# Feed-forward: how the 42 modulation chunks computed by GpSimd are summed over partitions, and how many may wait for their sum

## The chip, the cores and the metric

One core of a Trainium2 chip runs the whole program. The metric is the device time of one execution in microseconds (us). The engines are TensorE (PE in the profile, PEld for its weight loads), VectorE (DVE), ScalarE (ACT), GpSimd (POOL) and SyncE (SP), which issues most loads.

## The reference, cut to what matters

The model is two layers of a first block (token mixers, then a feed-forward with a short convolution) followed by two layers of a second block, on 512 tokens of 1024 features. Every layer is modulated by vectors that come from a product of a conditioning vector with a wide matrix:

```
mod = (cond @ w_ada[l] + b_ada[l])[:, None, :]
sh1, sc1, g1, sh2, sc2, g2 = jnp.split(mod, 6, axis=-1)
h = _rmsnorm(x, norm1_w[l]) * (1.0 + sc1) + sh1
x = x + g1 * _token_mixers(h, ...)
h = _rmsnorm(x, norm2_w[l]) * (1.0 + sc2) + sh2
x = x + g2 * _conv_ffn(h, ...)      # gelu(conv(h @ w_up) gate) * value @ w_down
```

`w_ada` is 1024 x 6144 for each layer of the first block and 1024 x 3072 for each of the second. The kernel cuts these products into chunks of 256 output columns. A few more products of the same kind ("shift" chunks) multiply the shift vector with the first columns of the next weight.

## The kernel before, in words

**Layout.** Activations are kept transposed: features on the 128 partitions, 512 tokens in the free dimension, 8 tiles `k` of 128 features. Every big product is made of three matmuls on rounded halves: an operand is split into a rounded high part (`hh`, `wh`, `fh`; by ScalarE) and the rounded rest (`hl`, `wl`, `fl`; by VectorE), and `thrice` issues high x high, high x low, low x high. In the profile all matmuls of these have line L560.

**Weights.** A piece of 1 MB of weights is loaded by SyncE into `raw` (2 buffers), ScalarE writes `wh`, VectorE writes `wl` by a subtraction of `wh` from `raw` (2 buffers each). TensorE then uses it for about 11 us. `Order.use(key)` marks the start of the use of a piece; it also places, in all engines' queues, the split of the next piece (`split_one`) and what comes with it.

**Feed-forward.** `order_ffn` writes the order by hand: 34 pieces, `up(0, 8)`, `up(8, 8)`, `down(0, 8)`, `up(16, 6)`, `down(1, 8)`, `down(2, 6)`. An up piece gives two channel tiles, in turn for the gate (`ug`) and the value (`uv`). Each tile goes through ScalarE (centre tap) and two VectorE instructions (outer taps, reading PSUM), then gelu on ScalarE, the product `ug<-ug,uv` on VectorE, and its split into `fh` and `fl`. A feed-forward begins with `order_early`: the first piece is multiplied with rows that are not yet normalised (`fh`, `fl` of `xT`), while VectorE and ScalarE make the normalised rows: for each of 8 tiles VectorE scales (`uv<-xT,acoef,rr`), ScalarE writes `hh`, VectorE writes `hl` (`hl<-uv,mod,hh`). TensorE's second piece waits for `hl` tile by tile.

**Modulation chunks.** During the two feed-forwards 42 chunks (25 in the first, 17 in the second) are computed by GpSimd, as unit `adap`. For each half of the 1024 rows: a multiplication by the conditioning vector (L1951, 128x1024), an addition (L1953, 128x512), then 128x256 additions (L1958, L1960, L1962) that leave in `adaacc` 128 partial sums for each of 256 columns. Behind each half it issues the load of the same half of the next chunk (L1934). The first chunk of a feed-forward waits for the last attention step of the block before (`s3`), so GpSimd begins well ahead of the feed-forward itself. A chunk's first write of `adaacc` (L1958) waits for the sum of the chunk that held the place before; there are two places.

**Sums.** Unit `adasum`: TensorE multiplies each half of `adaacc` as stationary operand with one column of ones (two float32 matmuls that write one column each), and VectorE adds the bias (`mod<-ps,sv`, 128x2). `Order.late` lists chunks whose sum is not yet placed. `split_one` places a sum when more than one chunk is late, `use` places all that were late at the use before, and `down` places what is left ahead of the first and the third down stage and at the end.

Of the kernel before, what the change touches and what calls it, by code (L numbers as in the profile page):

```python
# [107 lines left out]
class Memory:  # L108
    def __init__(self, nc, ctx):
        base = (nc.sbuf_base + 31) // 32 * 32  # L110
        top = nc.sbuf_usable_end // 32 * 32
        at = [base]
# [82 lines left out]
        self.strewn = [sb(f"strewn{i}", [128, 4, 256])[:, :, :] for i in range(2)]  # L195

# [43 lines left out]
    def mixer(self, nm, c):  # L240
# [6 lines left out]
        return y[:, c, :], high, low[:, c, :]  # L247

# [68 lines left out]
class Order:  # L317


    def __init__(self, plan):  # L320
        self.plan, self.units, self.split, self.used = plan, [], 0, 0
        self.late, self.old = [], 0
# [7 lines left out]

    def sums(self, n=None):
        for _ in range(len(self.late) if n is None else n):
            self.run(("adasum", self.late.pop(0)))
        self.old = 0

    def split_one(self):
# [5 lines left out]
        if self.plan[j]["kind"] == "ada":  # L342
# [3 lines left out]
            if len(self.late) > 1:  # L346
                self.run(("adasum", self.late.pop(0)))
                self.old = max(self.old - 1, 0)
# [7 lines left out]
    def use(self, key, alone=False):  # L356
# [6 lines left out]
        self.sums(self.old)  # L363
# [4 lines left out]
        while not alone and self.split <= then:  # L368
            self.split_one()
        return j  # L370
# [167 lines left out]
def tensor_program(e, X):  # L538
# [77 lines left out]
    def adasum(chunk_):  # L616
        b = take("side", ("ada", chunk_))
        acc = M.adaacc[X.acc[chunk_]]
# [300 lines left out]
def scalar_program(e, X):  # L919
# [47 lines left out]

    def split(j):
# [286 lines left out]
    def mixer_split(l, nm, c):  # L1255
        y, high, _ = M.mixer(nm, c)
        go.wait_ge(*at("gated", l, nm, c))
        if nm == "c":
            if c == 1 and l == 0:
                go.wait_ge(*at("sums", (2, 1, 11)))  # L1260
# [54 lines left out]
    parts = {"start": start, "loaded": loaded, "split": split, "sq": square, "sqf": first_square, "mod": modulate, "rms": inv_rms, "row": row,  # L1315
# [73 lines left out]
def vector_program(e, X):  # L1389
# [76 lines left out]

    def adasum(chunk_):
        which, l, j = chunk_
        if which == "shift":
# [10 lines left out]
    def ada_quick(n):  # L1480

        chunk_ = X.first[n]["chunk"]
        b = bank("ada", chunk_)
        sums, own = (b[:, c:c + 256].rearrange("p (x t) -> p x t", x=2) for c in (0, 256))
        dst, bias = M.mod1[:, 2 * chunk_[2]:2 * chunk_[2] + 2], M.vec("bada", 2 * chunk_[2], 2)
        go.wait_ge(*at("sums", chunk_))
        tt(own, sums, M.cst[:, C_ID:C_ID + 128].rearrange("p (x t) -> p x t", x=1).broadcast_to([128, 2, 128]), ALU.mult).then_inc(
            *up("dve_mod"))
        go.wait_ge(*last("dve_mod"))
        e.tensor_reduce(dst, own, mybir.AxisListType.X, ALU.add).then_inc(*up("dve_mod", ("out", ("ada", chunk_))))  # L1490
        go.wait_ge(*last("dve_mod"))
# [399 lines left out]
    parts = {"start": start, "loaded": loaded, "split": split, "ada0": ada_first, "adaq": ada_quick, "adaqm": ada_quick, "ada": ada, "adasum": adasum, "sq": square, "sqf": first_square,  # L1891
# [350 lines left out]
def order_ffn(o, l):  # L2242
# [19 lines left out]
    def down(gr, n, norm=None):  # L2262
        settle()
        if gr == 0:
            o.sums()
        if norm:
            tag = ("m1", 1) if l == 0 else ("m3", 0)
            o.sums()
            o.put("es", tag)
            o.put("lnexp")  # L2270
        for c in range(4):
            j = o.use(("down", l, gr, c))
            for x in range(2):
                o.put("down", l, gr, n, 2 * c + x, j)
# [330 lines left out]
```

## Time and profile before

| | |
|---|---|
| median of 3 runs | 2823.48 us (2821.91 to 2830.59) |
| the profiled execution | 2823.8 us, span 2822.0 us |
| TensorE busy | 2693.7 us (95% of the span) |
| VectorE, ScalarE, GpSimd busy | 1818.2, 1152.3, 693.9 us |
| granted TensorE clock, mean | 0.975 |
| chain that ended last | TensorE 85%, VectorE 7%, ScalarE 4% |

The first feed-forward lies at about 410 to 783 us of the span, the second at about 1134 to 1503 us. Where TensorE is busy without a gap, time changes only by the TensorE instructions that are added or removed and by waits that come to it from other engines.

### The profile page before, as it was taken

The page shows a single profiled execution, that of the slowest core. Times are in us where ns is not written, and L with a number is a line of the kernel's source. Part 1 is how long each engine was busy: PE and PEld are TensorE (multiplying, and loading weights), DVE is VectorE, ACT ScalarE, POOL GpSimd, SP SyncE. Part 2 cuts the span into 40 slices and gives each one's busy share as a digit, 9 for nine tenths or more (in the row PEclk, how much of TensorE's full clock was granted, in tenths as well). Part 3 has the DMA queues.
Part 4 walks back from the last instruction along what each step waited for, and adds up shares of the span by engine and source line. Part 5 has one row for each costly group of instructions (what it writes and reads, how often), then busy time and mean ns, then how long its engine had stood idle before and what let it go on. Part 6 is the DMA issues. An engine that isn't in the chain of part 4 may idle for free.

```text
span 2822.0 us, 36991 instructions
## 1 busy us (share of the span) xinstructions
PE 2693.7 (95%) x14886; PEld 2163.9 (77%) x14886; DVE 1818.2 (64%) x2968; ACT 1152.3 (41%) x1900; POOL 693.9 (25%) x514
## 2 busy tenths in 40 slices
PE   6999899999999998999998999989999999999997
PEld 5877578888878676888886878767687788777686
DVE  7789668867577676876558768645436557545434
ACT  3143544323243454533224463344324464444422
POOL 0000047988700004356540032000010132000110
PEclk9999999999999999999999999999899999999999
DMA  8353034554432212444433435221232323221231
GB/s 270 119 144 103 29 120 149 165 173 160 138 118 57 70 44 90 132 137 149 145 109 107 157 99 158 77 64 56 72 97 79 99 61 94 79 86 53 75 97 60
DMA packets 281114, 302.59 MB, mean 107 GB/s; under 512 B 9968, under 2 KB 263024, under 8 KB 280944
## 3 DMA queue, kind: packets, MB, share of 16 engines
q1 hardware_dynamic: 267568, 250.21, 28.4%
q0 software_dynamic: 13088, 49.55, 5.3%
q8 instruction: 118, 1.93, 0.3%
q10 hardware_dynamic: 288, 0.47, 0.0%
q14 instruction: 52, 0.43, 0.0%
HBM read 289.97 MB, written 2.10 MB: 103 GB/s over the span
## 4 chain that ended last, share of the span: by engine, by line
PE 85%; DVE 7%; ACT 4%; DMA 1%; issue 1%; SPq 0%; POOL 0%; DVEq 0%; ACTq 0%
PE ps L560 84%; PE ps L768 2%; DVE wl L1398 1%; DVE hl L1404 1%; DVE adaacc L1404 1%; DMA raw<-in_w_in 1%; DVE rawt L1404 0%; ACT wh L926 0%; DVE recat L1696 0%; ACT recat L926 0%; ACT hh L926 0%; DMA stage<-in_w_ada 0%; DMA t1s<-rawt 0%; ACT att_s L926 0%; ACT att_p L926 0%
## 5 line engine op out<-in xcount | busy, mean ns | idle before, releaser
L560 PE MATMUL ps<-hh,wh 128*128 128x512 f32 x2208 | 890.9, 403 | 24.8 <-DVE wl L1398 10.3
L560 PE MATMUL ps<-hh,wl 128*128 128x512 f32 x2208 | 868.0, 393 | 0.0
L560 PE MATMUL ps<-hl,wh 128*128 128x512 f32 x2208 | 867.2, 393 | 0.0
L1398 DVE TENSOR_TENSOR wl<-raw,wh 128x2048 fp32r<-128x2048 f32 (+3 forms) x234 | 501.2, 2150 | 208.1 <-ACT wh L926 207.8
L560 PEld LDWEIGHTS ps<-hh,wh 128*128 128x128 f32 x2208 | 417.6, 189 | 138.1 <-issue 39.6
L560 PEld LDWEIGHTS ps<-hh,wl 128*128 128x128 f32 x2208 | 417.6, 189 | 92.3
L560 PEld LDWEIGHTS ps<-hl,wh 128*128 128x128 f32 x2208 | 418.2, 189 | 81.2
L926 ACT ACTIVATE wh<-raw 128x2048 fp32r<-128x2048 f32 (+3 forms) x234 | 369.9, 1591 | 188.3 <-PE ps L560 172.8
L560 PE MATMUL ps<-fh,wh 128*128 128x512 f32 x432 | 171.6, 397 | 0.0
L560 PE MATMUL ps<-fh,wl 128*128 128x512 f32 x432 | 168.3, 390 | 0.0
L560 PE MATMUL ps<-fl,wh 128*128 128x512 f32 x432 | 168.1, 389 | 0.0
L1951 POOL TENSOR_TENSOR strewn<-strewn,cond 128x1024 f32<-128x1024 f32 x80 | 161.6, 2020 | 7.2 <-DMA strewn<-in_w_ada 5.4
L926 ACT ACTIVATE rawt<-ps 128x512 f32<-128x512 f32 (+1 forms) x106 | 63.1, 597 | 244.9 <-PE ps L560 244.7
L1404 DVE SCALAR_TENSOR_TENSOR xT<-ps,mod,xT 128x512 f32<-128x512 f32 x80 | 59.6, 748 | 146.8 <-PE ps L560 146.8
L1953 POOL TENSOR_TENSOR strewn<-strewn 128x512 f32<-128x512 f32 x84 | 150.2, 1788 | 6.6
L1977 POOL TENSOR_TENSOR merged<-merged,rawt 128x512 f32<-128x512 f32 x32 | 41.7, 1316 | 439.6 <-DVE rawt L1404 439.6
L1912 POOL DMA_DIRECT2D gbias<-in_gb x6 | 3.5, 577 | 552.7 <-DVE stt L1735 457.3
L560 PE MATMUL ps<-wh,hh 128*128 128x256 f32 x448 | 129.5, 289 | 3.3 <-DVE apad L1398 3.3
L560 PE MATMUL ps<-wh,hl 128*128 128x256 f32 x448 | 127.3, 284 | 0.0
L560 PE MATMUL ps<-wl,hh 128*128 128x256 f32 x448 | 127.3, 284 | 0.0
L560 PEld LDWEIGHTS ps<-recq,reck 64*128 64x128 f32 x1536 | 100.7, 200 | 29.0 <-issue 15.2
L560 PE MATMUL ps<-recq,reck 64*128 64x64 f32 (+2 forms) x1536 | 110.4, 295 | 7.2 <-DVE reck L1398 4.5
(291 smaller groups left out, 4157.0 us busy)
## 6 DMA issues: line engine op xcount, KB each, us to landing
raw<-in_w_in SPq DMA_DIRECT2D x75, 1024.0 KB, 5.4
raw<-in_w_up SPq DMA_DIRECT2D x46, 1024.0 KB, 5.1
strewn<-in_w_ada POOLq DMA_DIRECT2D x80, 512.0 KB, 4.1
raw<-in_w_ada SPq DMA_DIRECT2D x24, 1024.0 KB, 5.2
raw<-in_w_in SPq DMA_DIRECT2D x44, 512.0 KB, 5.1
raw<-in_w_out SPq DMA_DIRECT2D x16, 1024.0 KB, 5.1
raw<-in_w_down SPq DMA_DIRECT2D x16, 1024.0 KB, 5.2
stage<-in_w_ada SPq DMA_DIRECT2D x8, 1024.0 KB, 11.6
```

Source lines behind the costliest of these rows:

```text
L560: return e.matmul(o, a, b, start=start, stop=stop, skip_group_check=True)
L768: m = e.transpose(b[:, o:o + 128], S[:, 128 * x:128 * x + 128], M.ident)
L926: return e.activation(o, a, f, **k)
L1398: return e.tensor_tensor(o, a, b, op)
L1404: return e.scalar_tensor_tensor(out=o, in0=a, scalar=s, in1=b, op0=op0, op1=op1)
L1912: e.dma_start(M.Gb[h], X.T["gb"][2 * c + h, :, :]).then_inc(*X.tally.up16("bias_in", ("bias", l, c)))
L1951: e.tensor_tensor(v, v, weights, ALU.mult).then_inc(*up("pool_ada"))
L1953: e.tensor_tensor(v[:, 0:2, :], v[:, 0:2, :], v[:, 2:4, :], ALU.add).then_inc(*up("pool_ada"))
L1977: e.tensor_tensor(M.merged[:, o, :], M.merged[:, o, :], raw[:, :], ALU.add).then_inc(*up("pool_merge", ("merged", l, nm, o)))
```

## The change

The 42 chunks of the feed-forwards (`strewn`) are summed in another way. ScalarE copies the chunk's `adaacc` into a rounded `acc_high` (new unit `accs`), VectorE subtracts that from `adaacc` and leaves the rounded rest in the same place. TensorE multiplies a stationary matrix of minus ones with both (two matmuls with 256 moving columns each), so that each partition of the bank holds all 256 negated sums. VectorE multiplies them by the identity, reduces each row and subtracts the result from the bias. GpSimd has four places instead of two; the chunks that VectorE computes elsewhere keep two. The order of the sums changes: a chunk is halved (`halve`) at the end of a `use` when at least two chunks are late, and summed at the next `use`; nothing is flushed at the start of a down stage but what that stage needs. The chunks are strewn over 30 pieces instead of 32.

```diff
         self.strewn = [sb(f"strewn{i}", [128, 4, 256])[:, :, :] for i in range(2)]
+        self.acc_high = [sb(f"acchigh{i}", [128, 256], F32R) for i in range(2)]
+        self.adamore_r = rounded("adamore_r", [128, 512], at[0])
+        self.adaacc += [sb(f"adamore{i}", [128, 256]) for i in range(2)]
...
+    def halve(self):
+        if self.late and self.late[0] in self.strewn and self.late[0] != self.halved:
+            self.halved = self.late[0]
+            self.run(("accs", self.late[0]))
+
+    def sum_one(self):
+        self.halve()
+        self.run(("adasum", self.late.pop(0)))
...
     def split_one(self):
-            if len(self.late) > 1:
-                self.run(("adasum", self.late.pop(0)))
+            if len(self.late) > (3 if self.plan[j]["chunk"] in self.strewn else 1):
+                self.sum_one()
                 self.old = max(self.old - 1, 0)
...
     def use(self, key, alone=False):
         self.used += 1
-        self.sums(self.old)
+        if self.late and self.late[0] in self.strewn:
+            if self.halved == self.late[0]:
+                self.sum_one()
+        else:
+            self.sums(self.old)
         self.old = len(self.late)
         while self.split <= j:
             self.split_one()
...
+        if len(self.late) > 1:
+            self.halve()
         return j
...
     def adasum(chunk_):                      # TensorE
         b = take("side", ("ada", chunk_))
+        if chunk_ in X.strewn:
+            go.wait_ge(*at("rounded"))
+            go.wait_ge(*at("acc_low", chunk_))
+            high, low = M.acc_parts(X.acc[chunk_])
+            mm(b[:, 0:256], M.cst_r[:, C_NONE:C_NONE + 128], high, True, False)
+            mm(b[:, 0:256], M.cst_r[:, C_NONE:C_NONE + 128], low, False, True).then_inc(*up("pe_ada", ("sums", chunk_)))
+            return
...
+    def acc_split(chunk_):                   # ScalarE
+        go.wait_ge(*at("acc", chunk_))
+        act(M.acc_parts(X.acc[chunk_])[0], M.adaacc[X.acc[chunk_]][:, :], ACT.Copy).then_inc(*up("act_acc", ("acc_high", chunk_)))
...
+    def acc_split(chunk_):                   # VectorE
+        high, low = M.acc_parts(X.acc[chunk_])
+        go.wait_ge(*at("acc_high", chunk_))
+        tt(low, M.adaacc[X.acc[chunk_]][:, :], high.bitcast(F32), ALU.subtract).then_inc(*up("dve_acc", ("acc_low", chunk_)))
+
+    def own_sums(chunk_, dst, eye=M.ident):
+        sums, own, mask = M.diagonals(bank("ada", chunk_), eye)
+        go.wait_ge(*at("sums", chunk_))
+        tt(own, sums, mask, ALU.mult).then_inc(*up("dve_mod"))
+        go.wait_ge(*last("dve_mod"))
+        e.tensor_reduce(dst, own, mybir.AxisListType.X, ALU.add).then_inc(*up("dve_mod", ("out", ("ada", chunk_))))
+        go.wait_ge(*last("dve_mod"))
+
+    def strewn_sum(chunk_):
...
+        own_sums(chunk_, dst[:, col:col + 2])
+        tt(dst[:, col:col + 2], M.vec(bias, col, 2), dst[:, col:col + 2], ALU.subtract).then_inc(*up("dve_mod", ("mods", chunk_)))
...
     def down(gr, n, norm=None):
         settle()
-        if gr == 0:
-            o.sums()
+        while gr == 0 and any(c[:2] == (1, l) and c[2] >= 20 for c in o.late):
+            o.sum_one()
         if norm:
-            o.sums()
+            while any(c[:2] == ((1, 1) if l == 0 else (2, 0)) and c[2] < 8 for c in o.late):
+                o.sum_one()
...
                 o.put("down", l, gr, n, 2 * c + x, j)
+                if norm and c < 3 and x == 0:
+                    o.halve()
...
-        for n, c in enumerate(chunks):
-            self.acc[c], self.acc_before[c] = n % 2, chunks[n - 2] if n > 1 else None
+        ring, holder = [0, 0], {}
+        for c in chunks:
+            turn = 1 if c in self.strewn else 0
+            n = ring[turn] % (4 if turn else 2)
+            ring[turn] += 1
+            self.acc[c], self.acc_before[c], holder[n] = n, holder.get(n), c
...
-            (lambda: ffn(0), ada(1, 0, (5,)) + ada(1, 1, (1, 0, 2, 4)) + shift("m1", 1) + ada(1, 1, (3,)), 0, 32),
+            (lambda: ffn(0), ada(1, 0, (5,)) + ada(1, 1, (1, 0, 2, 4)) + shift("m1", 1) + ada(1, 1, (3,)), 0, 30),
-            (lambda: ffn(1), ada(1, 1, (5,)) + ada(2, 0, (1, 0, 2)) + shift("m3", 0), 0, 32),
+            (lambda: ffn(1), ada(1, 1, (5,)) + ada(2, 0, (1, 0, 2)) + shift("m3", 0), 0, 30),
```

## Rows read from the trace of the kernel before

**Rows 1.** The page: TensorE's busy time, and the other engines'.

```profile
PE 2693.7 (95%) x14886; PEld 2163.9 (77%) x14886; DVE 1818.2 (64%) x2968; ACT 1152.3 (41%) x1900; POOL 693.9 (25%) x514
```

**Rows 2.** Stretches: length; busy PE, PEld, DVE, ACT, POOL; clock; DMA share, GB/s.

```profile
456.00:592.00 136.00, 136.00 (x620) 112.92 (x618) 112.56 (x94) 50.95 (x61) 116.73 (x83) 1.00 0.51 167
834.00:845.00 11.00, 9.14 (x65) 8.66 (x65) 7.50 (x14) 2.78 (x3) 0.00 (x0) 0.69 0.35 95
```

**Rows 3.** The timeline of TensorE before and after one sum: start, duration, instruction.

```profile
456.23 0.39 PE L560 MATMUL ps<-hh,wl 128*128 128x512 f32 x1
...
459.68 0.39 PE L560 MATMUL ps<-hh,wh 128*128 128x512 f32 x1
```

**Rows 4.** The timeline of TensorE where matmuls of 256 columns follow ones of 512.

```profile
2246.42 0.39 PE L560 MATMUL ps<-hh,wl 128*128 128x512 f32 x1
...
2247.10 0.39 PE L560 MATMUL ps<-hh,wl 128*128 128x512 f32 x1
2247.32 0.28 PE L560 MATMUL ps<-wh,hh 128*128 128x256 f32 x1
2247.44 0.28 PE L560 MATMUL ps<-wl,hh 128*128 128x256 f32 x1
```

**Rows 5.** The timeline of GpSimd, 398 to 443 us; in brackets idle before and releaser.

```profile
400.47 1.63 POOL L1953 TENSOR_TENSOR strewn<-strewn 128x512 f32<-128x512 f32 x1
432.73 0.73 POOL L1958 TENSOR_TENSOR adaacc<-strewn 128x256 f32<-128x256 f32 x1 [30.64 <-PE ps L560]
...
439.09 1.06 POOL L1962 TENSOR_TENSOR adaacc<-adaacc,strewn 128x256 f32<-128x256 f32 x1
...
441.26 1.91 POOL L1951 TENSOR_TENSOR strewn<-strewn,cond 128x1024 f32<-128x1024 f32 x1
```

**Rows 6.** GpSimd's additions of 128x512, whole span: duration ns min/median/max.

```profile
L1953 POOL TENSOR_TENSOR strewn<-strewn x84: 1282/1627/3242, 373.0 to 1460.0; 128x512 f32<-128x512 f32 x84
```

**Rows 7.** The timeline of VectorE at the first feed-forward's start.

```profile
412.43 2.29 DVE L1398 TENSOR_TENSOR wl<-raw,wh 128x2048 fp32r<-128x2048 f32 x1 [1.05 <-ACT wh L926]
414.64 1.41 DVE L1404 SCALAR_TENSOR_TENSOR uv<-xT,acoef,rr 128x512 f32<-128x512 f32 x2
...
424.14 1.63 DVE L1404 SCALAR_TENSOR_TENSOR hl<-uv,mod,hh 128x512 fp32r<-128x512 f32 x2
```

**Rows 8.** The timeline of TensorE, the end of the same stretch.

```profile
425.83 0.50 PE L560 MATMUL ps<-hh,wh 128*128 128x512 f32 x1
...
432.08 0.95 PE L560 MATMUL ps<-cst,adaacc 128*128 128x1 f32 x8
```

**Rows 9.** The timeline of VectorE while GpSimd works, beside rows 5.

```profile
438.58 0.97 DVE L1398 TENSOR_TENSOR ug<-ug,uv 128x512 f32<-128x512 f32 x1
439.48 1.22 DVE L1398 TENSOR_TENSOR fl<-ug,fh 128x512 fp32r<-128x512 f32 x1
...
440.76 4.57 DVE L1398 TENSOR_TENSOR wl<-raw,wh 128x2048 fp32r<-128x2048 f32 x1
```

**Rows 10.** VectorE's instructions on `xT`, whole span: duration ns min/median/max.

```profile
L1404 DVE SCALAR_TENSOR_TENSOR xT<-ps,mod,xT x80: 733/750/752, 374.6 to 2806.9; 128x512 f32<-128x512 f32 x80
...
L1404 DVE SCALAR_TENSOR_TENSOR fl<-xT,acoef,fh x40: 737/747/2754, 376.7 to 2174.1; 128x512 fp32r<-128x512 f32 x40
L1404 DVE SCALAR_TENSOR_TENSOR uv<-xT,acoef,rr x16: 741/744/747, 414.6 to 1147.3; 128x512 f32<-128x512 f32 x16
```

**Rows 11.** The timeline of all engines at the second feed-forward's start.

```profile
1147.93 1.63 DVE L1404 SCALAR_TENSOR_TENSOR hl<-uv,mod,hh 128x512 fp32r<-128x512 f32 x2
...
1155.87 0.50 PE L560 MATMUL ps<-cst,adaacc 128*128 128x1 f32 x4
...
1156.51 0.74 POOL L1958 TENSOR_TENSOR adaacc<-strewn 128x256 f32<-128x256 f32 x1 [30.53 <-PE ps L560]
```

**Rows 12.** The timeline of TensorE, its one long wait in an up stage.

```profile
445.47 0.47 PE L560 MATMUL ps<-hh,wh 128*128 128x512 f32 x1 [1.40 <-DVE wl L1398]
```

**Rows 13.** VectorE by group, 10 to 60 us: busy, mean ns of one.

```profile
L1398 DVE TENSOR_TENSOR ps<-ps,cst 128x256 f32<-128x256 f32 x4 | 1.7, 426 | 0.0
```

More of the change, by code:

```diff
@@ L247, in mixer, with acc_parts, diagonals @@
         return y[:, c, :], high, low[:, c, :]
+    def acc_parts(self, n):
+        low = self.adaacc_r if n < 2 else self.adamore_r
+        return self.acc_high[n % 2][:, :], low[:, 256 * (n % 2):256 * (n % 2) + 256]
+    def diagonals(self, b, eye):
+        sums, own = (b[:, c:c + 256].rearrange("p (x t) -> p x t", x=2) for c in (0, 256))
+        return sums, own, eye.rearrange("p (x t) -> p x t", x=1).broadcast_to([128, 2, 128])
     def split_parts(self, p):
@@ L321, in __init__ @@
         self.plan, self.units, self.split, self.used = plan, [], 0, 0
-        self.late, self.old = [], 0
+        self.late, self.old, self.halved = [], 0, None
+        self.strewn = {p["chunk"] for p in plan if p["strewn"]}
         self.main_free, self.side_free, self.split_end = [0.0], [0.0], {}
@@ L1313, in index_scores @@
             *up("act_index", ("out", ("ts", l, i, h)), ("relu", l, i, h)))
-    parts = {"start": start, "loaded": loaded, "split": split, "sq": square, "sqf": first_square, "mod": modulate, "rms": inv_rms, "row": row,
+    parts = {"start": start, "loaded": loaded, "split": split, "accs": acc_split, "sq": square, "sqf": first_square, "mod": modulate, "rms": inv_rms, "row": row,
              "er": early_row, "em": early_mend, "z": z, "q": q, "iv": iv, "g": g, "qk": qk, "a": a, "zs": gates, "rd": rec_diagonal, "rl": rec_level, "ra": rec_across, "ro": rec_out,
@@ L1465, in ada @@
         products(p["chunk"], M.piece(M.raw[p["slot"]], p, 0))
+    def acc_split(chunk_):
[10 more added lines that the diff above has]
+    def strewn_sum(chunk_):
+        which, l, j = chunk_
+        go.wait_ge(*at("rounded"))
+        if which == "shift":
+            dst = M.shifted((l, j))
+            own_sums(chunk_, dst)
+            ts(dst, dst, -1.0, None, ALU.mult).then_inc(*up("dve_mod", ("mods", chunk_)))
+            return
+        dst, bias, per = (M.mod1, "bada", 48) if which == 1 else (M.mod2, "bada2", 24)
+        col = l * per + 2 * j
+        own_sums(chunk_, dst[:, col:col + 2])
+        tt(dst[:, col:col + 2], M.vec(bias, col, 2), dst[:, col:col + 2], ALU.subtract).then_inc(*up("dve_mod", ("mods", chunk_)))
     def adasum(chunk_):
         which, l, j = chunk_
+        if chunk_ in X.strewn:
+            strewn_sum(chunk_)
+            return
         if which == "shift":
@@ L1482, in ada_quick @@
         chunk_ = X.first[n]["chunk"]
-        b = bank("ada", chunk_)
-        sums, own = (b[:, c:c + 256].rearrange("p (x t) -> p x t", x=2) for c in (0, 256))
         dst, bias = M.mod1[:, 2 * chunk_[2]:2 * chunk_[2] + 2], M.vec("bada", 2 * chunk_[2], 2)
[L1486 to L1491, printed above, removed]
+        own_sums(chunk_, dst, M.cst[:, C_ID:C_ID + 128])
         tt(dst, dst, bias, ALU.add).then_inc(*up("dve_mod", ("mods", chunk_)))
@@ L2404, in __init__ @@
         self.first = first_chunks(T)
+        self.strewn = {p["chunk"] for p in self.plan if p["strewn"]}
         self.order = make_order(Order(self.plan), self.first)
```

6 lines of the change are left out of this document (3 added, 3 removed).

## The prediction

> **What bounds the kernel.** I read the page first: TensorE is busy 95% of the span [rows 1]. The waits within the feed-forwards come next; in the table by stretch TensorE is busy for all of the 136 us of the up pieces, while VectorE has 23.4 us to spare and GpSimd 19.3 [rows 2]. So here a change counts for what it adds to or takes from TensorE's own queue, and for what it makes late enough to stop TensorE. For the first I read the timeline of TensorE around one sum. For the second I read three timelines side by side at the start of a feed-forward, because that is the one place there where VectorE sets TensorE's pace: the last `hl` tile is written by 425.77 (424.14 plus 1.63) and the matmul that needs it starts at 425.83; TensorE then has the rest of that piece before it and comes to the next one, with its first sum, at 432.08 [rows 7, 8]. The same 6.3 us stand in the second feed-forward: 1149.56 to 1155.87 [rows 11]. Nothing is to spare: each microsecond by which the last `hl` comes later is one of the total.
>
> **Removed: the float32 sums on TensorE.** The matmul at 459.68 is the 13th of 512 columns behind the one at 456.23, and one sum lies between them, so without it they would be 13 plain steps apart [rows 3]. The plain step is 0.227: three of them lie between 2246.42 and 2247.10 [rows 4]. So a sum costs 3.45 - 13 x 0.227 = 0.50 us (the record of its four parts alone has 0.50 too [rows 11], but overlaps its neighbours), its slow start and the slow steps behind it included. 42 chunks would be 21.2; four pairs placed together (one is the x8 row of 0.95 [rows 8]) are a little cheaper. I take 21.0.
>
> **Added: two matmuls of 256 columns.** The trace has no sum of this kind, but matmuls of this form and size, started 0.12 apart, right behind one of 512 at no extra cost [rows 4]: 0.24 for two. The return to 512 columns may add some hundredths; upper bound, the plain step twice, 0.45. I take 0.26: 42 x 0.26 = 10.9. TensorE's own account: 21.0 - 10.9 = 10 us gained (bounds 2 and 11).
>
> **Added on VectorE.** For each chunk: the product with the identity, known from the first chunks, 0.43 [rows 13], and for the reduction of the same 256 values I take the same; the last small instruction takes the place of the bias addition. That is 0.86 less overlap, 0.8. The subtraction that makes the low half is 128x256; between nothing and the 0.75 of a 128x512 with two inputs in SBUF [rows 10], I take 0.4. It reads two operands in SBUF, and such instructions are lengthened while GpSimd works (below), by 0.7 in the second and 2.3 in the third of [rows 9], against 0.55 (below) and 2.29 [rows 7] alone: with 0.8 for that, 1.2. So 2.0 us a chunk. In the up stages there are 10 chunks for 12 pieces, 20 us against 23.4 idle [rows 2]. Queued behind the added instructions on VectorE is the `wl` of the next piece, and TensorE waits for that; it does so already once, 1.40 us, behind a `wl` that took 4.57 [rows 9, 12]. With 0.8 more ahead of each `wl` I expect that wait to be 0.8 longer and a few of a microsecond or less in the first feed-forward's up stages: 3 us (0 if the spare time takes it all; 9 if each of the 18 later up pieces loses 0.5). In the down stages VectorE waits for TensorE and the work is covered. In the second feed-forward chunks are a third fewer: nothing. ScalarE's copy is covered: that engine is idle for 85 of the 136 us [rows 2]. That ScalarE is held by a chunk that GpSimd has not finished costs nothing as long as GpSimd is ahead, and by the next paragraph it is up to four chunks ahead; if that cover went, `wh` of the next piece would be late.
>
> **Moved: GpSimd runs ahead.** Before, GpSimd finishes two chunks, does the first half of the third up to 402.1 and then waits 30.64 us, until TensorE's first sum at 432, for a place [rows 5]. It waits the same way, 30.53, in the second feed-forward [rows 11]. These two waits cover exactly the stretches in which VectorE writes `uv` and `hl` (412.4 to 425.8 [rows 7], and up to 1149.6 [rows 11]). With four places the third and fourth chunk need no sum, and GpSimd stops only at its fifth chunk's first write. From 402 on it finishes the third chunk (its second half, to about 410), then does the fourth and the first two instructions of the fifth. The change also puts the first sum no earlier.
>
> What that does to VectorE is in two timelines side by side. GpSimd's instruction of 439.09 takes 1.06 where one of its size alone takes 0.73, and ends at 440.15, 0.6 behind VectorE's end at 439.55. VectorE's next, started at 439.48 without a gap, ends at 440.70, 0.55 behind GpSimd's. The `wl` at 440.76 ends 2.2 behind GpSimd's 1.91 [rows 5, 9]. The two take turns, one whole instruction each, even where VectorE's follow each other without a gap. Which of VectorE's do so: `xT<-ps,mod,xT`, one input in PSUM, never exceeds 752 ns in 80; `fl<-xT,acoef,fh`, both in SBUF, goes to 2754; `uv<-xT,acoef,rr`, of the same form, has 747 at most, but only because GpSimd stood still in all 16 [rows 10]. The Trainium skill, in "SBUF — State Buffer", section "Who interferes with whom", states this as an exclusive lock: a VectorE instruction with two inputs in SBUF and a GpSimd instruction that reads SBUF block each other for the whole instruction, and one with at most one such input doesn't. By that rule the trace agrees, and it speaks against this change: all 16 `uv` and `hl` instructions have two inputs in SBUF. Without it the sum below would be -7.
>
> The price: behind 412.4 GpSimd still has the fourth chunk, 1.9 + 1.3 + 0.73 for the first half and 1.9 + 1.3 + 0.73 + 0.73 for the second, 8.6 us, and 3.2 of the fifth; less up to 2 done by then, 10 to 12 us [rows 5, 6]. VectorE has 17 instructions in a row there (one `wl`, 8 `uv`, 8 `hl` [rows 7]), more than GpSimd's nine, so nearly every one of GpSimd's gets its turn between two of VectorE's. Some fall into time in which VectorE would wait for ScalarE's `hh`. I step through both queues taking turns and get 8 to 11 us for the last `hl`, and take 9 in each feed-forward: 18 us. Bounds: 0 and 12 each. Nothing takes this up later, as TensorE goes on without a gap.
>
> **The clock.** While TensorE waits for `hl` eight times it is busy about a third of the time. After a gap of similar idleness the granted clock falls: 0.69 over 834 to 845 us, where TensorE was busy 9.14 of 11 behind a wait [rows 2]; half the clock, the 1.2 GHz level, for 6.8 us of that. What of such a stretch falls into the waiting is free; what falls into the 24 last matmuls of the piece costs their 5.4 us again at most. I take 1 us each, 2 in all (0 to 10).
>
> **The sum**, against the profiled execution's 2823.8 us (the median is 0.3 lower): -10 + 3 + 9 + 9 + 2 = +13, so 2837 us.
>
> **Rivals.**
> *Faster: the modulation keeps its pace.* If GpSimd's instructions are the ones that yield while VectorE's follow each other closely, or GpSimd is held elsewhere (a load that lands late), the last `hl` stays at 425.8. Then -10 + 1 to 3: 2815 us. For it: `uv` to `hl` start 0.67 apart while they last 0.745 (two in 1.41 [rows 7]), so VectorE's overlap. Against it: so did the pair at 438.58 and 439.48, and GpSimd came between. It decides if the two stretches grow by less than 1.5 us together. Chance 0.12.
> *About the same: half the collisions.* Each of GpSimd's instructions delays, but VectorE gets two or three turns for one, or GpSimd is itself slowed so much in the out stage that it starts its fourth chunk late: 4 to 6 us each, and no clock loss: -10 + 2 + 10 = +2, 2826 us. Chance 0.22.
> *VectorE becomes the bound of the up stages as well.* 20 us on 23.4 idle leaves little, and the chunks come 32/30 more densely: every up piece of the first feed-forward then waits up to a microsecond, 12 instead of 3: 2846 us. Chance 0.10.
> *The change does not do what it says:* excluded as far as the places go, since nothing holds the third and fourth place.
>
> **Chances and range.** My forecast has 0.56. What a measurement of this kernel can tell is about 0.3%, 8.5 us: faster is below 2815, slower above 2832. From the faster rival 0.08 falls below that, 0.04 within; the halved one lies within for 0.19 and above for 0.03; forecast and saturation are above but for 0.05. Faster 0.08, same 0.28, slower 0.64. The range reaches from between the first two rivals to beyond the third: 2817 to 2850; the forecast's own is 2829 to 2848.
>
> **What the profile after would show.** GpSimd's wait of 30.6 at L1958 gone at the third chunk and found, shorter, at the fifth; `uv<-xT` and `hl<-uv` with maxima near 2.7 us; the last `hl` near 435 instead of 425.8; TensorE waiting eight times in that piece, a clock below 1.00 there; sums as pairs of 256-column matmuls with the next start 0.24 to 0.27 later; `wl` in the up stages ending closer to its use. I am wrong if the last `hl` stays within 2 us of where it was, if a sum still costs TensorE over 0.4, or if TensorE's waits for `wl` in the up stages exceed 9 us.

## The result, and where the 29 us lie

| | before | after |
|---|---|---|
| median (range) | 2823.3 us (2821.91 to 2830.59) | 2852.24 us (2845.16 to 2857.23) |
| the profiled execution | 2823.8 us, span 2822.0 | 2852.12 us, span 2850.3 |

The ratio is 1.0095, with an interval of 1.0068 to 1.0123: slower, as forecast, but by 29 us instead of 13, and just outside the range (2850). The medians are of four executions each; the page ahead of the prediction had the first three of the kernel before (2823.48). One execution of all those told of below, of e4_hold_psum, took 9208 us; without it that kernel's median would be 0.1 us lower.

The page of the changed kernel, beside [rows 1]:

```profile
PE 2696.4 (95%) x14802; PEld 2158.4 (76%) x14802; DVE 1913.6 (67%) x3094; ACT 1166.6 (41%) x1942; POOL 702.5 (25%) x514
```

TensorE's busy time grew by 2.7 us only, the span by 28.3: most of what was added is waiting. To see where, I used a landmark: four matmuls `ps<-nrm,cst` begin each stage of the program. In TensorE's timeline of the kernel before, the first feed-forward begins with this row:

```profile
409.31 1.98 PE L560 MATMUL ps<-nrm,cst 128*128 128x512 f32 x4
```

and in the changed kernel the first and the second begin with these:

```profile
411.73 1.98 PE L590 MATMUL ps<-nrm,cst 128*128 128x512 f32 x4 [1.32 <-DVE nrm L1439]
...
1152.36 1.98 PE L590 MATMUL ps<-nrm,cst 128*128 128x512 f32 x4 [1.07 <-DVE nrm L1439]
```

From such a row to the next one there is one feed-forward with what belongs to it. Stretch by stretch (starts of those rows, differences worked out):

```
                         before    after    difference
to the 1st feed-forward   409.3    411.7      +2.4
the 1st feed-forward      376.0    395.7     +19.7
the block between         347.8    344.9      -2.9
the 2nd feed-forward      371.3    380.1      +8.8
behind it, two stretches 1303.9   1304.2      +0.3
```

So the two feed-forwards have 28.5 us, all of the span's 28.3. The rest moves by some microseconds either way from trace to trace, also between kernels that are alike there.

**The start of the first feed-forward.** The timeline of VectorE in the changed kernel; before, each `uv` and `hl` had about 0.745 [rows 7, 10]. A row with x2 is two instructions:

```profile
414.85 3.73 DVE L1439 TENSOR_TENSOR wl<-raw,wh 128x2048 fp32r<-128x2048 f32 x1 [0.90 <-ACT wh L963]
418.50 2.92 DVE L1445 SCALAR_TENSOR_TENSOR uv<-xT,acoef,rr 128x512 f32<-128x512 f32 x2
421.35 3.11 DVE L1445 SCALAR_TENSOR_TENSOR hl<-uv,mod,hh 128x512 fp32r<-128x512 f32 x1
...
427.20 1.21 DVE L1445 SCALAR_TENSOR_TENSOR uv<-xT,acoef,rr 128x512 f32<-128x512 f32 x1
428.33 3.10 DVE L1445 SCALAR_TENSOR_TENSOR hl<-uv,mod,hh 128x512 fp32r<-128x512 f32 x1
...
437.01 1.62 DVE L1445 SCALAR_TENSOR_TENSOR hl<-uv,mod,hh 128x512 fp32r<-128x512 f32 x2
```

The timeline of GpSimd beside it:

```profile
428.16 0.79 POOL L1997 DMA_DIRECT2D strewn<-in_w_ada  x1 [0.30 <-POOL adamore L2025]
428.97 1.91 POOL L2014 TENSOR_TENSOR strewn<-strewn,cond 128x1024 f32<-128x1024 f32 x1
430.96 1.61 POOL L2016 TENSOR_TENSOR strewn<-strewn 128x512 f32<-128x512 f32 x1
446.03 0.75 POOL L2021 TENSOR_TENSOR adaacc<-strewn 128x256 f32<-128x256 f32 x1 [13.46 <-PE ps L590]
```

And TensorE, which waits for those `hl`, and reaches the next piece, with its first sum, at 445.41 (432.08 before [rows 8]):

```profile
427.33 0.50 PE L590 MATMUL ps<-hh,wh 128*128 128x512 f32 x1 [1.84 <-DVE hl L1445]
431.49 0.80 PE L590 MATMUL ps<-hh,wh 128*128 128x512 f32 x1 [3.20 <-DVE hl L1445]
...
445.41 0.36 PE L590 MATMUL ps<-acchigh,cst_r 128*128 128x256 f32 x1
```

The reader is to see three things. GpSimd's wait of 30.64 us at the third chunk [rows 5] is gone, and a wait of 13.46 stands at the fifth. As long as GpSimd works, `uv` and `hl` last 1.2 to 3.1 us; from 433.04 on, behind its last instruction, they last 0.74 again. And the last `hl` comes at 438.64 (437.01 plus 1.62), 26.9 us behind the norm's sum, where it was 16.5 (425.77 less 409.3); in the second feed-forward 27.7, where it was 16.5. That is 10.4 and 11.2 us.

**The up stages.** The waits of TensorE in the changed kernel, 410 to 800 us: in total, times, longest.

```profile
PE ps L590 <- DVE hl L1445: 5.7, 3, 3.2
PE ps L590 <- DVE adaacc_r L1439: 5.4, 3, 3.5
PE ps L590 <- DVE adamore_r L1439: 2.8, 2, 1.5
PE ps L590 <- DVE wl L1439: 2.0, 1, 2.0
```

`adaacc_r` and `adamore_r` are the rounded rests of the chunks. TensorE waits more for these than for `wl`. Here is the largest of those waits, from both sides; VectorE first:

```profile
454.85 1.66 DVE L1439 TENSOR_TENSOR mod<-sv,mod 128x2 f32<-128x2 f32 x1
456.44 2.28 DVE L1439 TENSOR_TENSOR wl<-raw,wh 128x2048 fp32r<-128x2048 f32 x1
458.64 1.49 DVE L1439 TENSOR_TENSOR adaacc_r<-adaacc,acchigh 128x256 fp32r<-128x256 f32 x1
```

```profile
456.42 0.39 PE L590 MATMUL ps<-hh,wl 128*128 128x512 f32 x1
460.27 0.55 PE L590 MATMUL ps<-acchigh,cst_r 128*128 128x256 f32 x1 [3.47 <-DVE adaacc_r L1439]
460.62 0.42 PE L590 MATMUL ps<-adaacc_r,cst_r 128*128 128x256 f32 x1
460.84 0.63 PE L590 MATMUL ps<-hh,wh 128*128 128x512 f32 x1
461.27 0.63 PE L590 MATMUL ps<-hl,wh 128*128 128x512 f32 x1
```

The sum stands in TensorE's queue ahead of the next piece, and its rounded rest stands in VectorE's queue behind that piece's `wl`. So TensorE stops until the rest is written, at 460.13 (458.64 plus 1.49), though `wl` was there at 458.7. Two more things are in these rows. An instruction of 128x2 took 1.66 us. And the matmuls behind the stop start 0.43 apart (460.84, 461.27) instead of 0.23: the clock was at its lower level, 1.2 GHz. The table by stretch gives the clock granted in the changed kernel at the first feed-forward's start and around this stop (length; busy PE, PEld, DVE, ACT, POOL; clock; DMA share, GB/s):

```profile
429.00:440.00 11.00, 7.82 (x20) 5.11 (x21) 10.87 (x13) 5.21 (x7) 3.49 (x2) 0.55 0.15 49
457.00:467.00 10.00, 6.72 (x19) 5.42 (x20) 9.86 (x11) 4.42 (x6) 8.18 (x6) 0.66 0.49 159
```

Within the first feed-forward half the clock was granted for 10.2 us from 429, for 6.8 from 459 and for 3.4 from 627.

**The sums.** An undisturbed one, in TensorE's timeline:

```profile
474.01 0.40 PE L590 MATMUL ps<-hh,wl 128*128 128x512 f32 x1
474.24 0.28 PE L590 MATMUL ps<-acchigh,cst_r 128*128 128x256 f32 x1
474.36 0.29 PE L590 MATMUL ps<-adamore_r,cst_r 128*128 128x256 f32 x1
474.48 0.40 PE L590 MATMUL ps<-hh,wh 128*128 128x512 f32 x1
...
477.23 0.39 PE L590 MATMUL ps<-hh,wh 128*128 128x512 f32 x1
```

The last row is the 13th of 512 columns behind the first, with one sum between: 3.22 - 13 x 0.227 = 0.27 us (3.22 is 477.23 less 474.01), against 0.50 before.

### The profile page after: what moved, and what is told of

Same layout as the page of the kernel before. It is cut to its first block, busy times and chain, and to the rows that moved or that the text cites. A ratio compares the mean times of both kernels' runs of the same rounds, so it can differ in the third digit from the quotient of the medians.

```text
span 2850.3 us, 36978 instructions
## 1 busy us (share of the span) xinstructions
PE 2696.4 (95%) x14802; PEld 2158.4 (76%) x14802; DVE 1913.6 (67%) x3094; ACT 1166.6 (41%) x1942; POOL 702.5 (25%) x514
## 4 chain that ended last, share of the span: by engine, by line
PE 79%; DVE 14%; ACT 4%; issue 2%; DMA 1%; SPq 0%; DVEq 0%; ACTq 0%
PE ps L590 78%; DVE wl L1439 2%; PE ps L805 2%; DVE hl L1445 1%; DVE uv L1445 1%; DVE fl L1439 1%; DVE ug L1439 1%; DVE adaacc L1445 1%; DVE ug L1445 1%; DMA raw<-in_w_in 0%; DVE rawt L1445 0%; DVE recat L1759 0%; ACT wh L963 0%; DVE fl L1445 0%; DVE xT L1445 0%
## 5 line engine op out<-in xcount | busy, mean ns | idle before, releaser
L1439 DVE TENSOR_TENSOR wl<-raw,wh 128x2048 fp32r<-128x2048 f32 (+3 forms) x234 | 470.5, 2019 | 198.0 <-ACT wh L963 197.8
L2016 POOL TENSOR_TENSOR strewn<-strewn 128x512 f32<-128x512 f32 x84 | 156.6, 1864 | 6.6
```

The source lines that it names most:

```text
L1439: return e.tensor_tensor(o, a, b, op)
L2016: e.tensor_tensor(v[:, 0:2, :], v[:, 0:2, :], v[:, 2:4, :], ALU.add).then_inc(*up("pool_ada"))
```

## The experiments

All were timed beside the kernel before, in three groups (e1 to e4, e5 to e8, e9 and e10), each on one chip; there the kernel before had 2824.16, 2823.81 and 2825.65 us. The ratio is to the kernel before of the same group, so kernels of different groups are better compared by their ratios. "GpSimd held" means: the third chunk's first write of its place also waits for the last `hl` of the feed-forward. FF1 and FF2 are the two feed-forwards, from norm sum to norm sum; "last hl" is from the norm sum to its end in each. These are read from one profiled execution of each kernel, which was up to 8 us faster than the kernel's median (e6: 2817.86 against 2825.83); outside the feed-forwards a stretch differs by up to 5 us from before. So the two feed-forwards show where time went, and the medians how much it was.

```
kernel                               median   ratio (95%)              FF1    FF2    last hl
before                               2823.3                            376.0  371.3  16.5 16.5
after                                2852.2   1.0095 (1.0068-1.0123)   395.7  380.1  26.9 27.7
e1_hold          after, held         2829.06  1.0013 (1.0002-1.0024)   388.1  370.9  16.5 16.5
e2_places        before, 4 places    2851.3   1.0100 (1.0085-1.0115)   385.1  384.6  26.9 27.7
e3_float_sums    after, old sums     2850.47  1.0094 (1.0080-1.0109)   385.3  382.6  26.9 27.7
e4_hold_psum     e1, small tiles     2830.43  1.0023 (1.0011-1.0035)   382.7  370.7  16.4 16.5
e5_later_sums    e4, sum a use later 2818.52  0.9978 (0.9966-0.9990)   376.4  367.4  16.5 16.5
e6_places_hold   e2, held            2825.83  1.0001 (0.9990-1.0012)   377.0  371.3  16.5 16.5
e7_high_only     e1, no rounded rest 2812.04  0.9957 (0.9941-0.9973)   370.9  365.2  16.5 16.5
e8_float_hold    e3, held            2826.17  1.0003 (0.9991-1.0014)   378.9  371.4  16.4 16.5
e9_release_432   e5, held less       2813.89  0.9961 (0.9948-0.9975)   373.6  367.4  16.5 16.5
e10_release_441  e5, held more       2823.3   0.9991 (0.9979-1.0004)   381.0  368.1  16.5 16.4
```

**e1_hold: the change, with GpSimd held.**

```diff
     def ada(j):                              # GpSimd
+        since[0] = 0 if p["first"] else since[0] + 1
...
+                if since[0] == 2:
+                    go.wait_ge(*at("hl", ("m2", p["layer"]), KD - 1))
```

> The changed kernel, with one wait added: GpSimd's first write of adaacc for the third chunk of each feed-forward waits for the last hl tile of that feed-forward's modulation. Four places, halves and the order of sums stay. Theory 1 (GpSimd running ahead takes turns with the 16 uv and hl instructions, and this is most of the loss): the last hl comes within 1 us of where it was before, the clock falls at 429 and 1166 us go away, and the time falls by 22 to 30 us to 2822 to 2830. Rival (the sums' extra work on VectorE in the up stages is most of the loss): under 8 us gained, 2844 or more.

Measured: 2829.06 us, 23 less than after. The last `hl` is back at 16.5 in both feed-forwards, and the second feed-forward is at 370.9. But the first is at 388.1, 12 more than before although its 25 sums are cheaper by 6. TensorE's waits there, 405 to 795 us, are for the rounded rests:

```profile
PE ps L590 <- DVE adaacc_r L1439: 8.4, 4, 3.4
PE ps L590 <- DVE adamore_r L1439: 2.7, 2, 1.4
PE ps L590 <- DVE wl L1439: 1.4, 2, 1.1
```

So there are two losses, and the hold takes away one of them. In this feed-forward half the clock was granted three times, for 3.4 us each, next to stops of 3.36, 2.06 and 2.47 us for rounded rests.

**e2_places: the kernel before, with the four places alone.** No new sums, no rounded halves, the old order.

```diff
+        self.adaacc += [sb(f"adamore{i}", [128, 256]) for i in range(2)]
...
-        for n, c in enumerate(chunks):
-            self.acc[c], self.acc_before[c] = n % 2, chunks[n - 2] if n > 1 else None
+        strewn = {p["chunk"] for p in self.plan if p["strewn"]}
+        ring, holder = [0, 0], {}
+        for c in chunks:
+            turn = 1 if c in strewn else 0
+            n = ring[turn] % (4 if turn else 2)
+            ring[turn] += 1
+            self.acc[c], self.acc_before[c], holder[n] = n, holder.get(n), c
```

> The kernel before with four places for the feed-forwards' chunks instead of two and nothing else: float32 sums, their order and the 32 pieces as before. Theory 1: GpSimd runs ahead here too, the last hl is 10 to 13 us late in each feed-forward, with a half-clock stretch behind it, and the time is 2844 to 2852. Rival (the loss needs the new sums): within 5 us of before.

Measured: 2851.3 us. Two more places, and nothing else, cost about as much as the whole change. Its last `hl` comes at the same 26.9 and 27.7. From the norm sum to the first sum behind that piece it is 33.5 and 34.0 us, where both were 22.8 before: 10.8 and 11.2 lost. (In its trace the span is 27.5 us longer than before; 22.4 of that lie in the two feed-forwards, 4.6 in the block between them, which is left open.) A matmul of it that waited for `hl`:

```profile
430.44 0.80 PE L561 MATMUL ps<-hh,wh 128*128 128x512 f32 x1 [3.19 <-DVE hl L1405]
```

**e3_float_sums: the change, but with the old sums** (no rounded halves; new places, order and 30 pieces).

```diff
-            self.run(("accs", self.late[0]))
...
-        if chunk_ in X.strewn:                   # TensorE
+        if False:
...
-        if chunk_ in X.strewn:                   # VectorE
-            strewn_sum(chunk_)
-            return
```

> The changed kernel with the old arithmetic of the sums: no ScalarE copy, no low half, two float32 matmuls with one column of ones, one 128x2 bias addition; places, strewing over 30 pieces and the position of each sum stay. Theory 1 plus what the changed kernel's trace shows (TensorE waits for adaacc_r of 1.3 to 3.9 us, about 11 us with a clock fall of 3 more, against 10 us gained by cheaper matmuls): TensorE's waits before sums go, each sum costs 0.50 again, total 2846 to 2853. Rival (the sums' work on VectorE is most of the loss): under 2838.

Measured: 2850.47 us, like the change. TensorE waits for no sum's operand any more, but the last `hl` is as late as there, and the 10 us of the cheaper sums are missing. So the new sums as a whole bring nothing here: they save 10 on TensorE and lose about as much again. (That is by the medians. The profiled execution of e3 took 2846.22 us, 4 less than its median, and its feed-forwards are 7.9 us shorter together than those of the changed kernel.)

**e4_hold_psum: e1 with the small results in PSUM.** I had overlooked `mod<-sv,mod`, the last small instruction of a new sum, 128x2 with both inputs in SBUF. In the changed kernel its group reads (duration min/median/max in ns)

```profile
L1439 DVE TENSOR_TENSOR mod<-sv,mod x40: 160/332/2490, 454.9 to 1498.8; 128x2 f32<-128x2 f32 x40
```

```diff
-        own_sums(chunk_, dst[:, col:col + 2])
-        tt(dst[:, col:col + 2], M.vec(bias, col, 2), dst[:, col:col + 2], ALU.subtract).then_inc(*up("dve_mod", ("mods", chunk_)))
+        b = bank("ada", chunk_)
...
+        e.tensor_reduce(b[:, 0:2], own, mybir.AxisListType.X, ALU.add).then_inc(*up("dve_mod"))
+        go.wait_ge(*last("dve_mod"))
+        tt(dst[:, col:col + 2], M.vec(bias, col, 2), b[:, 0:2], ALU.subtract).then_inc(
+            *up("dve_mod", ("out", ("ada", chunk_)), ("mods", chunk_)))
```

> The hold of e1_hold, and the reduction leaves its result in PSUM, so that the last 128x2 subtraction has one SBUF input instead of two. In the changed kernel's trace that instruction takes 0.86 us on average, up to 2.49, while GpSimd works, and 0.16 alone. If that wait comes from the second SBUF input, it is 0.15 throughout here, wl and the low half end 0.7 us sooner, and the time is 2 to 6 us below e1_hold. If VectorE has room enough in the up stages, the two are equal.

With one input in PSUM none of these instructions is lengthened (over all 40 the mean was 0.69 us in the changed kernel, not the 0.86 of the expectation):

```profile
L1439 DVE TENSOR_TENSOR mod<-sv,ps x40: 156/156/157, 441.6 to 1474.6; 128x2 f32<-128x2 f32 x40
```

In the trace the first feed-forward is 5.4 us shorter than e1's, but the medians do not differ (2830.43 and 2829.06; the expectation had 2 to 6 us less). For the total it is inconclusive. By the rule of the Trainium skill, "SBUF — State Buffer", section "Who interferes with whom", a VectorE instruction with at most one input in SBUF, outside the modes in which it uses both ports, does not contend with GpSimd; the trace agrees, with 0.156 to 0.157 us in all 40.

**e5_later_sums: e4, with each sum one use later than its halves.** The rounded rest then has a whole piece to arrive.

```diff
     def use(self, key, alone=False):
+        self.turn += 1
...
-            if self.halved == self.late[0]:
+            if self.half and self.half[0] < self.turn - 1:
                 self.sum_one()
...
-        if len(self.late) > 1:
+        if len(self.late) > len(self.half) + 1:
             self.halve()
...
```

> e4_hold_psum with each feed-forward sum placed one piece later than its halves (two uses behind the halving instead of one, up to two chunks halved at a time), so that the low half, queued on VectorE behind the next wl, has 11 us more before TensorE asks for it. Theory 2 (what e1 still loses is TensorE's own queue stopped by a low half that VectorE has not reached): TensorE's waits for adaacc_r and adamore_r, 12 us with the clock falls behind them in e4, go; the first feed-forward takes 372 to 377 us between the two norm sums instead of 382.7, and the second 368 to 370. Rival (VectorE simply has too much to do there): TensorE waits as long, now for wl, and the time stays that of e4.

Measured: 2818.52 us, 0.2% below before: its interval does not reach 1, but it is less than the 0.3% that I set as the mark. Against e4 it is 12 us less by the medians, and the intervals of the two ratios lie apart; the first feed-forward is 6.3 us shorter in the traces. The waits for rounded rests are gone (8.0 us in e4's first feed-forward). TensorE goes through the sum and stops for `wl` instead, 5.3 us in all where e4 had 0.8, so part of what the rival expected came true:

```profile
438.05 0.28 PE L595 MATMUL ps<-adaacc_r,cst_r 128*128 128x256 f32 x1
441.49 0.47 PE L595 MATMUL ps<-hh,wh 128*128 128x512 f32 x1 [3.17 <-DVE wl L1446]
```

VectorE of the same kernel shows why that `wl` is late: GpSimd, let go at the last `hl`, works there too, and each of these instructions met it.

```profile
429.93 2.58 DVE L1446 TENSOR_TENSOR ug<-ug,uv 128x512 f32<-128x512 f32 x1
...
434.96 3.10 DVE L1446 TENSOR_TENSOR fl<-ug,fh 128x512 fp32r<-128x512 f32 x1
437.99 3.35 DVE L1446 TENSOR_TENSOR wl<-raw,wh 128x2048 fp32r<-128x2048 f32 x1
```

**e6_places_hold: e2 with the hold of e1.** Are four places harmful in themselves?

```diff
+                if since[0] == 2:
+                    go.wait_ge(*at("hl", ("m2", p["layer"]), KD - 1))
```

> e2_places (the kernel before with four places) plus the hold of e1: GpSimd's third chunk of each feed-forward waits for the last hl tile. Theory 1: the places cost nothing by themselves, so this is the kernel before again, 2819 to 2829, both feed-forwards within 1 us of 376.0 and 371.3. Rival (four places lengthen VectorE's instructions all through the feed-forwards): 5 us or more above before.

Measured: 2825.83 us, as before; both feed-forwards are within 1 us of before (377.0 and 371.3). The places cost nothing; what GpSimd does with them at that moment does.

**e7_high_only: e1 without the rounded rest.** One matmul on the high half alone, and no subtraction on VectorE. It leaves the rounded rest out of the sums.

```diff
-            go.wait_ge(*at("acc_low", chunk_))
+            go.wait_ge(*at("acc_high", chunk_))
...
-            mm(b[:, 0:256], M.cst_r[:, C_NONE:C_NONE + 128], high, True, False)
-            mm(b[:, 0:256], M.cst_r[:, C_NONE:C_NONE + 128], low, False, True).then_inc(*up("pe_ada", ("sums", chunk_)))
+            mm(b[:, 0:256], M.cst_r[:, C_NONE:C_NONE + 128], high, True, True).then_inc(*up("pe_ada", ("sums", chunk_)))
...
```

> e1_hold without the low half: VectorE's subtraction is gone and TensorE multiplies the high half alone, which leaves out the rounded rest of each of the 42 chunks' partial sums. TensorE then waits for ScalarE's copy only. Theory 2: TensorE's waits before sums go, a sum costs about 0.15 us instead of 0.27, VectorE has 0.4 to 1.4 us less for each chunk; first feed-forward 366 to 371 us instead of 388.1, in all 2806 to 2814. If the product, the reduction and the contended 128x2 subtraction are what VectorE is short of, most of the 12 us stay as waits for wl.

Measured: 2812.04 us, 17 less than e1. The first feed-forward is 17.2 us shorter. The matmul that is missing accounts for 25 x 0.12 = 3.0 of that, so the rounded rest, its lateness and VectorE's work for it together, cost 14. This run takes load from VectorE as well, so by itself it does not tell the lateness from the load; e5 does. In the second feed-forward it is 5.7, of which 17 x 0.12 = 2.0 are the matmuls. (Outside the feed-forwards e7's trace is 8 us longer than e1's, for which I have no cause.)

**e8_float_hold: e3 with the hold.** The old sums, with the places, the order and the 30 pieces of the change:

```diff
-        if chunk_ in X.strewn:
+        if False:
...
+                if since[0] == 2:
+                    go.wait_ge(*at("hl", ("m2", p["layer"]), KD - 1))
```

> e3_float_sums plus the hold of e1: four places, the new positions of the sums and 30 pieces, but the old float32 arithmetic, and GpSimd held off the modulation. It differs from e1 in the sums' arithmetic alone. Theory 1: 2820 to 2828, both feed-forwards as before. Then e1 against it shows what the halves give: 10 us less for cheaper matmuls, 12 to 20 more for waits and clock in the first feed-forward, about 4 less in the second.

Measured: 2826.17 us. The order and the places of the change without its arithmetic are as before. Its first feed-forward is 378.9, its second 371.4; e1, which differs only by the sums' arithmetic, has 388.1 and 370.9. So under the hold the halves cost 9.2 us in the first and gain 0.5 in the second, where cheaper matmuls alone would give 5.9 and 4.0; by the ratios (1.0013 and 1.0003) e1 loses 0.1%, about 3 us.

**e9_release_432 and e10_release_441: e5, with GpSimd let go later.** The wait for the last `hl` is replaced by one for a tile that VectorE finishes in the first piece of the up stage, or for one in the next.

```diff
-                    go.wait_ge(*at("hl", ("m2", p["layer"]), KD - 1))
+                    go.wait_ge(*at("conv3", ("ug", p["layer"], 1)))      # e9
+                    go.wait_ge(*at("fl", p["layer"], 1))                 # e10
```

> e5_later_sums with the hold on GpSimd ended a little later: its third chunk's first write of adaacc waits for the second gate tile's convolution on VectorE (about 7 us behind the last hl) instead of for the last hl. In e5 TensorE still stops 3.4 us for the wl of the fourth piece, behind a product, an fl and the wl itself, each lengthened by 1.1 to 2.4 us. If that is GpSimd's taking turns, part of those instructions stays contended here, and the stop is 1 to 3 us; total within 2 us of e5.

> e5_later_sums with the hold ended behind the second fl tile, just ahead of the wl that TensorE stops for. If turn-taking makes that stop, only the wl itself can be contended: the stop is under 1.5 us, no clock fall behind it, first feed-forward 372 to 375 us instead of 376.4, total 2 to 5 us below e5. Rival: GpSimd now starts too late, ScalarE waits for the third chunk ahead of its halving, and wh and wl of the next pieces come late: TensorE's waits move there, total as e5 or above.

e9 measured 2813.89 us, 0.4% less than before and 38 less than after: the fastest kernel here that does the whole computation (e7 leaves a part out). It is 4.6 us below e5, where I expected at most 2, but the intervals of the two ratios overlap. Its stop at the same place is halved,

```profile
439.45 0.28 PE L595 MATMUL ps<-adaacc_r,cst_r 128*128 128x256 f32 x1
441.37 0.47 PE L595 MATMUL ps<-hh,wh 128*128 128x512 f32 x1 [1.64 <-DVE wl L1446]
```

and no stretch of its feed-forwards has the lower clock. e10 measured 2823.3 us, no gain; here the rival of the expectation came true. Its first feed-forward is at 381.0, with 8.2 us of waits for `wl` (4.0 in e9), the longest of 3.30. Held that long, GpSimd is no longer ahead, and ScalarE, which copies the high half in its own queue, waits for it, 39.7 us in all against 18.2 in e9 (400 to 790 us):

```profile
ACT acchigh L968 <- POOL adamore L2044: 24.7, 6, 8.6
ACT acchigh L968 <- POOL adaacc L2044: 15.0, 4, 6.8
```

The prediction had named the danger: if GpSimd's lead went, `wh` of the next piece would be late.

## Why the prediction was right in direction and wrong in size

The terms of the prediction's sum, beside what each measured:

```
term                               predicted   measured   from
cheaper sums on TensorE               -10        -9.9     42 x (0.506 - 0.27); 0.506 is the 0.50 with the plain step at 0.2267
last hl later, 1st feed-forward        +9  }
last hl later, 2nd feed-forward        +9  }    +22.1     10.9 + 11.2, norm sum to next piece or to last hl
the clock at the two starts            +2  }
VectorE in the up stages               +3       +16.3     what is left: 14.7 + 1.6
sum                                   +13       +28.5     the feed-forwards: +28.5
```

What is left is worked out so, from the stretches' differences: 19.7 - 10.9 + 25 x 0.236 = 14.7 in the first feed-forward, 8.8 - 11.2 + 17 x 0.236 = 1.6 in the second.

**The sum on TensorE: right.** 0.27 us for a pair against 0.26 in the prediction.

**GpSimd running ahead: right, and a little small.** The place, the mechanism (one whole instruction in turn) and the victim were as foreseen, and e2 shows that the places alone do it, e6 that the hold alone undoes it. The last `hl` comes 10.4 and 11.2 us later, where I stepped through to 8 to 11 and took 9. What the stepping had left out is in the rows above: the `hl` of 428.33 was also held while GpSimd issued a load (428.16 to 428.95), and through the instruction behind it until 430.88, 3.10 us in all; the one of 421.35 likewise. I had let the loads' issues pass as free, though [rows 9] has such a case.

**The clock at the starts: small, as foreseen.** Half the clock was granted for 10.2 us and 13.7 us, a lot more than I imagined, yet nearly all of it fell into the waiting for `hl`: in the first feed-forward the step from the norm sum to the next piece grew by 10.9, the last `hl` by 10.4. There it cost about half a microsecond, where I took one.

**VectorE in the up stages: this is the step that failed.** The prediction says: "Queued behind the added instructions on VectorE is the `wl` of the next piece, and TensorE waits for that". It looked for the load that the new instructions put on VectorE (20 us against 23.4 idle) and for what stands behind them. It did not ask for the deadline of the new instructions themselves. TensorE's sum is in order with its other work, and the rounded rest that it needs is the last in VectorE's queue, behind `wl`. Where the sum has 3 us for this, 14.7 + 1.6 = 16.3 were lost. Of the 14.7 us in the first feed-forward 8.8 are longer waits (5.4 + 2.8 + 2.0, less 1.4 [rows 12]), and most of the rest fits the lower clock next to two stops, one for a rest and one for `wl`: 6.8 and 3.4 us at half of it, 5.1 us if TensorE was busy throughout (an estimate). Four observations bear this out. The waits name the rounded rests. Without that half (e7) 14 us go. With the sum a piece later (e5) the waits for it are gone, and the first feed-forward falls from 382.7 to 376.4. And with the old sums (e8), where TensorE needs no rest, the first feed-forward is 9.2 us shorter than in e1.

The order in the queue is not all of it. With the cheaper sums and nothing lost, the first feed-forward would be at 376.0 - 5.9 = 370.1; e4 loses 12.6 us against that and e5 still 6.3, with 5.3 us of waits for `wl`. In e6 and e8, which have the hold and the old sums, such waits are 2.4 and 2.5 us. So about half of e4's loss was the missed deadline; the other half stays with `wl`, which GpSimd's instructions and the sums' extra work on VectorE both delay. How these two share it was not separated.

None of the three signs of being wrong came: the last `hl` did move, a sum costs TensorE 0.27 us, and its waits for `wl` in the first feed-forward were 2.0 us, not over 9. They watched `wl`, while the longest stops were for the rounded rests. Of the other signs, `hl` reached 3.12 us and `uv` 1.77 where both were to come near 2.7.

**The rival "VectorE becomes the bound": its number came closer than mine, its reason was not the right one.** It gave 12 us for the first feed-forward. But VectorE is not full there: the table by stretch has for the changed kernel

```profile
456.00:592.00 136.00, 130.21 (x569) 107.02 (x568) 122.57 (x121) 54.23 (x70) 117.05 (x82) 0.97 0.49 162
474.00:592.00 118.00, 115.68 (x517) 95.46 (x516) 104.93 (x105) 48.29 (x62) 101.43 (x72) 1.00 0.48 158
```

VectorE has 13.4 us idle in the first row and 13.1 in the second, while TensorE is idle for 5.8 and 2.3. The order in the queue makes about half of the loss: e5 moves the sums only and has 6.3 us less.

**The rivals on the other side:** the modulation did not keep its pace and the collisions were not halved. e1 shows what would have come had it kept its pace: 2829 us, not the 2815 of the faster rival, which had the same step wrong. That this lies near the 2826 of the halved rival is chance.

**Left open.** How much of e4's 5.4 us in one trace is real; how the waits for `wl` that e5 keeps divide between GpSimd and the sums' work on VectorE; whether the 1.3 us and 1.1 us by which `nrm` comes late at the norm sums of the changed kernel have their own cause or are collisions of the same kind; and why a stretch outside the feed-forwards moves by up to 5 us from trace to trace.

## What to carry to other kernels

A buffer more for an engine off the critical path is a change of its schedule: ask where it will now be working and which instructions of the critical engine's supplier stand there. Here four places alone cost 27 us, and one wait more, until the last `hl`, brought it to nothing. And when work is moved into pieces (a half made by one engine, summed by another), the piece last in the supplier's queue sets the time: look up its deadline in the consumer's order, not only the supplier's load. Give it a whole step of slack before removing instructions.

## What the runs showed of the hardware

- A VectorE instruction of 128x2 with both inputs in SBUF took 0.16 us in the 10 of 40 cases in which it met no instruction of GpSimd but the issue of a load, or none at all, and 0.29 to 2.49 us in the 30 others, nearly as long as a 128x512 one in the same trouble (up to 3.1); with one of the inputs in PSUM it took 0.156 to 0.157 in all 40.
- A VectorE instruction with two inputs in SBUF that starts while GpSimd issues a load usually stays blocked until the end of GpSimd's next instruction, and then ends 0.56 us behind it (a `wl` 2.16). So an `hl`, `fl` or `ug` that starts early in the issue takes up to 3.1 us instead of 0.7, more than the 1.91 us of the instruction that it meets. The two feed-forwards of the trace after have 28 such starts of `hl`, `fl`, `wl` and `ug<-ug,uv`, 22 of them lengthened so; those of the trace before have 17, 14 of them lengthened (the `wl` of 4.57 in [rows 9] is one). In three of the six undisturbed cases of the trace after, all of them `wl`, GpSimd's next instruction took 3.2 us instead of 1.91: there it was GpSimd that waited. What decides between the two is open.
- Stops of TensorE of 3.2 to 3.5 us for an operand from VectorE in an up or down stage came with 3.4 to 6.8 us at half the clock in after, e1, e4, e5 and e10, but one of 3.15 us in e7 did not. Of stops of about 2 us some did (2.06 in e1, 1.98 in after and in e4) and some did not (2.09 in e9). So the length of the stop alone does not decide.
- Two 256-column matmuls of rounded operands cost TensorE 0.27 us in a row of 512-column ones, the four float32 one-column parts 0.50.
